# One fixed place for the split weights, and the next stage's first two blocks rounded and parted in four more tails

## What is computed

```
x = first_block(x, p, ...)
for i in range(4):
    h = modulate(rmsnorm(x, norm_g[i]), shift, scale)
    y = conv_branch(h) | rwkv_mixer(h) | attn_mixer(h)     # i = 0 and 3 | 1 | 2
    x = x + gate * y
return rmsnorm(x, final_g)
```

## Time and profile before

| | us |
|---|---|
| median of three runs | 3019.34 |
| lowest, highest | 3016.89, 3021.15 |
| the profiled execution: its own time | 3007.58 |
| its span, first to last instruction | 3005.8 |
| PE busy (28252 matmuls) | 2610.2 (87%) |
| PE weight loads | 2028.2 (67%) |
| DVE busy | 1748.8 (58%) |
| ACT busy | 1122.0 (37%) |
| POOL busy | 776.2 (26%) |
| mean granted clock of PE, share of full speed | 0.936 |

### The profile page before, as it was taken

How to read it: one execution, slowest core, us unless ns; L and a number is a source line. 1 busy time by engine, 2 the same in 40 slices (tenths; PEclk the granted TensorE clock), 3 DMA queues, 4 the chain that set the end, 5 groups by cost and what they waited for, 6 DMA issues and landing times. The chain is left out here.

```text
span 3005.8 us, 65971 instructions
## 1 busy us (share of the span) xinstructions
PE 2610.2 (87%) x28252; PEld 2028.2 (67%) x28252; DVE 1748.8 (58%) x2951; ACT 1122.0 (37%) x1751; POOL 776.2 (26%) x437
## 2 busy tenths in 40 slices
PE   7896879998599997788888888678999999898987
PEld 5774658776487686677677777567778755476755
DVE  4646978977822675454554554354771066535995
ACT  4531332223333422444444443332442344333323
POOL 2322210001122123644444452122332300032111
PEclk9998989989698898899999999889999999999998
DMA  4214424432234455111111100324332200033431
GB/s 149 77 43 133 161 71 118 111 93 91 97 107 151 157 188 182 40 36 45 51 40 46 51 25 14 122 91 147 133 126 64 84 1 1 1 119 92 136 94 56
DMA packets 83662, 266.34 MB, mean 89 GB/s; under 512 B 11824, under 2 KB 12848, under 8 KB 82992
## 3 DMA queue, kind: packets, MB, share of 16 engines
q1 hardware_dynamic: 74160, 236.97, 24.8%
q10 hardware_dynamic: 9216, 25.17, 2.1%
HBM read 203.04 MB, written 36.70 MB: 80 GB/s over the span
## 5 line engine op out<-in xcount | busy, mean ns | idle before, releaser
L358 PE MATMUL ps<-h_parts_conv,w_parts_conv 128*128 128x512 f32 x3936 | 766.5, 356 | 83.7 <-DVE h_parts_conv L344 47.6
L358 PEld LDWEIGHTS ps<-h_parts_conv,w_parts_conv 128*128 128x128 f32 x3936 | 643.2, 193 | 212.9 <-issue 54.7
L358 PE MATMUL ps<-scratch_scan 64*64 64x64 f32 (+1 forms) x15936 | 379.8, 239 | 82.9 <-issue 44.5
L358 PEld LDWEIGHTS ps<-scratch_scan 64*64 64x64 f32 x15936 | 342.9, 140 | 127.5 <-issue 83.6
L355 ACT ACTIVATE scratch_scan<-ps 128x384 f32<-128x384 f32 x560 | 241.0, 493 | 370.5 <-PE ps L358 228.4
L358 PE MATMUL ps<-h_parts_attn,w_parts_attn 128*128 128x512 f32 (+1 forms) x1536 | 330.5, 374 | 19.9 <-DVE h_parts_attn L352 12.3
L352 DVE SCALAR_TENSOR_TENSOR scratch_conv<-scratch_conv,vec 128x256 f32<-128x256 f32 (+1 forms) x672 | 335.2, 572 | 0.5
L358 PEld LDWEIGHTS ps<-h_parts_attn,w_parts_attn 128*128 128x128 f32 x1536 | 264.6, 191 | 78.6 <-issue 15.2
L432 POOL TENSOR_TENSOR w_parts_conv<-ring,w_parts_conv 128x1024 fp32r<-128x1024 f32 x50 | 131.4, 2629 | 592.2 <-ACT w_parts_conv L355 592.2
L358 PE MATMUL ps<-h_parts_block,w_parts_block 128*128 128x512 f32 x960 | 243.7, 414 | 38.5 <-POOL w_parts_block L432 27.7
L358 PEld LDWEIGHTS ps<-h_parts_block,w_parts_block 128*128 128x128 f32 x960 | 189.4, 200 | 92.4 <-issue 42.8
(11 more groups left out here) (206 smaller groups left out, 3586.0 us busy)
## 6 DMA issues: line engine op xcount, KB each, us to landing
ring<-in_weights SPq DMA_DIRECT2D x311, 512.0 KB, 3.7
rwkv_spill<-scratch_conv ACTq DMA_DIRECT2D x64, 384.0 KB, 2.3
stream<-rwkv_spill SPq DMA_DIRECT2D x64, 384.0 KB, 4.0
scratch_conv<-scratch_conv SPq DMA_DIRECT2D x128, 103.1 KB, 2.2
scratch_conv<-scratch_conv SPq DMA_DIRECT2D x128, 67.4 KB, 2.0
x_spill<-stream SPq DMA_DIRECT2D x2, 3072.0 KB, 9.7
y_spill<-scratch_scan SPq DMA_DIRECT2D x8, 384.0 KB, 4.0
scratch_rwkv_out<-y_spill SPq DMA_DIRECT2D x8, 384.0 KB, 6.5
```

What stands on the lines that cost most here:

```text
L358: return nc.tensor.matmul(o, l, r, start=start, stop=stop)
```

## The change

The split weights get a scope of their own, opened before everything else, so that they lie at one address. Only a stage with `split=False` (the scan) closes it; the stage after it opens it again. The softmax stage's scratch gets smaller by the size of the split weights (4096 elements per partition), since they now stay in place through it. With that, gate1, rwkvout, attn and attnout round (ACT) and part (POOL) the first two blocks of the next dense stage as well: their limits rise by two. The calls at the head of conv0, attn, attnout and conv1 stay in the code and find nothing left to do.

```diff
-        kept_scope, area_scope, parts_scope = (ctx.enter_context(ExitStack()) for _ in range(3))
+        w_scope, kept_scope, area_scope, parts_scope = (ctx.enter_context(ExitStack()) for _ in range(4))
...
             area_scope.close()
+            if not split:
+                w_scope.close()
+                PARTS.pop("W")
+            elif "W" not in PARTS:
+                weight_parts(name)
...
-            PARTS["W"] = ap(parts_scope.enter_context(nc.sbuf_tensor(f"w_parts_{name}", [P, 2, 2, DT * P], F32R)))
+        def weight_parts(name):
+            PARTS["W"] = ap(w_scope.enter_context(nc.sbuf_tensor(f"w_parts_{name}", [P, 2, 2, DT * P], F32R)))
...
+        weight_parts("one")
...
-                part_block(g, PSTART["gate1"] + DT)
+                part_block(g, PSTART["gate1"] + DT + 2)
...
-                    round_block(a, PSTART["gate1"] + min(m + 3, DT))
+                    round_block(a, PSTART["gate1"] + m + 3)
...
-        add_products("rwkvout", TT, lambda m, c: MODL[:, 1, 16 + m, c:c + 1], 0,
+        add_products("rwkvout", TT, lambda m, c: MODL[:, 1, 16 + m, c:c + 1], 2,
...
-        limit = PSTART["attnout"]
+        limit = PSTART["attnout"] + 2
...
-        area("parts", "softmax", SPLIT)
+        area("parts", "softmax", SPLIT - 4 * DT * P)
...
-                        round_block(a, min(PSTART["attnout"] + 2 * m + half + 3, PSTART["conv1"]))
+                        round_block(a, PSTART["attnout"] + 2 * m + half + 3)
...
-                part_block(g, PSTART["conv1"])
+                part_block(g, PSTART["conv1"] + 2)
```

## The result

The change made the kernel slower: 3028.24 us, median of 11 runs (3024.07 to 3038.84), against 3019.40 us of before (11 runs, 3016.89 to 3022.25); ratio 1.0026, 95% interval 1.0016 to 1.0037. The prediction said 3019.2 and a range up to 3025.5. The profiled execution after took 3033.27 us (span 3031.5).

The account below looks back on a forecast made before the run. PE, busy in 87% of the span, sets the pace in dense stages; the change moves its stops between stages. Tails 13.8 less heads 13.9 is -0.1 us, so 3019.2 on the runs' scale, range 3012.5 to 3025.5.

Parts of the forecast that it names:

- The fixed address and the smaller softmax scratch change no instruction: nothing: Whole kernel: the new place of the split weights and the smaller softmax scratch cost 0 us.
- The heads: Starts of conv0, attn, attnout, conv1: without two roundings and two partings each, 2.8, 3.0, 5.5, 2.6 saved, 13.9 us together.
- Conv1's head: Start of conv1: PE's third slice at 2744.0 in place of 2746.54, 2.6 us saved.
- the memset alone: Starts of conv0 and conv1: POOL's memset moves up against DVE's first low parts and costs nothing there.
- The tails: Ends of gate1, rwkvout, attn, attnout: added roundings and partings cost 3.7, 2.9, 3.9, 3.3, together 13.8 us.
- the 0.6 for the clock: End of rwkvout: PE's four sums take 2.93 in place of 2.32 us after a longer stop, 0.6 added.
- the clock's share: Start of softmax: PE's first 8 matmuls may run at half clock, 1.8 us more, of which 1.0 was taken.
- The tails are nearly free: Rival, all four tails: they cost 1.0, 1.0, 2.9 and 1.0 us, giving -8.0 and 3011.3; chance 0.13.
- The longer stops cost PE its clock: Rival, softmax's start, attnout's head, first dense blocks of conv0, attn, conv1: half clock, +6.3 us, 3025.6; chance 0.12.
- The blocks aren't there in time: Rival, end of gate1: a rounding waits for its load, one load late giving +3.7 us, 3023; chance 0.03.

Follow-up runs that it names:

- two gaps: Kernel after with 192 empty bytes behind the split weights and 64 ahead of attnout's split inputs, all stages aligned to 256: 3016.97 us, ratio 1.0008 to before.
- the gap of 64 in the kernel before: Kernel before with 64 empty bytes between split inputs and split weights, nothing else changed: ratio 1.0048 to before.
- the placement alone: Kernel after with all four added preparations undone, only the new fixed place of the split weights kept: 3023.86 us beside 3015.86 of before, ratio 1.0023.
- the aligned one: Kernel after without its four preparations, with 448 empty bytes behind the split weights and 576 ahead of attnout's split inputs: ratio 1.0007 to before.
- the second profile of before: Kernel before run once more unchanged for another profile: 3018.21 us.
- the two kernels after with a gap of 64 or 448: Kernel after with 64 or 448 empty bytes behind the split weights: ratios 1.0026 and 1.0009 to before.

## Why the prediction was wrong

**The step that failed** is the one sentence "The fixed address and the smaller softmax scratch change no instruction: nothing". It is true that they change no instruction, and it doesn't follow that they cost nothing. Timed alone they cost 0.23% [0.12, 0.35] of about 3016, some 7 us; with the distance mended 0.07% [-0.06, 0.19]. The same from the other side: the kernel after goes from 1.0026 to 1.0008 with two gaps, some 5 us of its 8.8. An upper estimate of the size comes from the rows: 44.51 less 44.10 over 192 is 2.1 ns for a matmul of 512. Blocks of 512 columns with a bad distance are 72 (in1, out1, gate1, conv1, convout1) and 32 in attn; 104 x 24 matmuls x 2.1 ns are 5.2 us. In attn's 16 wider blocks a pair of 512 and 256 takes some 1.5 ns longer (352.0 and 352.3 in the two kernels with the bad distance, 350.5 to 350.9 in before and the aligned ones, each the mean of a profile), 0.6 us. Together 5.8, if PE sets the pace all through; the 74 wider blocks of the other stages are left out, since their pace has two values of its own (below). For the gap of 64 in the kernel before, the same working (6.6 ns, attnout's 16 blocks too, 2.5 ns a pair in attn) gives 20, of which 14.5 were measured. PE does not set the pace everywhere: conv1's last dense product ends 164.45 us behind the stage's start in the placement alone and 164.30 in the aligned one, where its 576 matmuls at 2.1 ns would make 1.2 us.

**The heads** were right in sum. The timelines of the placement alone and of the kernel after, and those of the same two aligned, agree on it. Conv0's last dense product comes 2.9 us sooner behind the stage's start (2.8 said), in both pairs; attnout's comes 5.5 and 5.6 sooner (5.5 said), conv1's 1.9 and 2.0 (2.6 said), and attn's first product 3.1 (3.0 said). Together that is 13.5 in place of 13.9. Conv1's head was mis-sized by 0.7: POOL's building of the diagonals comes forward too (2766.31, behind the memset) and holds DVE's first low part for 1.38 us in place of 0.74. The prediction counted the memset alone and not what POOL does next. The stage times are a poorer measure: conv0 as a whole is 2.8 shorter in the aligned pair and 0.3 longer in the other, all of it behind its dense products, and of the 4.3 that conv1 to convout1 gained only 1.4 to 1.9 are in conv1; the rest lies in the two stages behind it, in which no instruction changed.

**The tails** came out at 13.8, as said, with errors that cancel; that is luck in part. Gate1 cost 3.5 to 3.7 by the stage times (3.7 said). Attnout cost 3.7 (3.3 said), by its timeline after against the aligned placement alone: from DVE's addition of the last product to PE's sums 4.93 and 2.20 us, and for the sums 2.07 and 1.13. Rwkvout cost 2.2 to 2.3 by the stage times (2.9 said), and the term that failed is the 0.6 for the clock: the sums took 2.93 after the longer stop, but without preparation, after the same stop of 3.23, they took 2.32 only in the first profile of before:

```profile
2011.50 2.93 PE L358 MATMUL ps<-scratch_rwkv_out,con 128*128 128x512 f32 x4 [3.23 <-DVE scratch_rwkv_out L344]
```

That is the second profile of before; the other kernels without this preparation have 2.27 to 2.93. At the start of softmax PE stood 3.92 us in place of 0.94, 3.0 more (2.9 said), and the clock's share was 1.2 us (1.0 said; 2.1 in the two kernels after with a gap of 64 or 448). The twentieth reduction of DVE in softmax starts 64.93 us behind PE's first product before and 66.09 after, and the distance between the two kernels is the same all the way from the fortieth matmul on:

```profile
2462.05 0.96 DVE L2827 TENSOR_REDUCE scratch_softmax<-ps 128x1 f32<-128x768 f32 x1 [5.05 <-PE ps L358]
```

```profile
2490.90 0.96 DVE L2836 TENSOR_REDUCE scratch_softmax<-ps 128x1 f32<-128x768 f32 x1 [5.05 <-PE ps L366]
```

Here the clock did fall: in the 4.2 us from 2424.8 on the granted clock was 0.72 and then 0.50, where before had 1.00. Attn with softmax should have grown by 0.9 in all (3.9 less 3.0); it grew by 7.2 in the pair that isn't aligned and by 0.4 in the aligned one. The softmax stage grew alike in both (2.4 and 2.3), so it is attn's own length that isn't settled: 4.8 longer in one pair, 1.9 shorter in the other.

**The rivals.** "The tails are nearly free" fell with the row of rwkvout. "The longer stops cost PE its clock" gave 3025.6, closer to the time than the forecast, but for the wrong reason, and that it came closer is luck: the granted clock over the whole span is 0.933 after and 0.933 in the second profile of before, and the aligned kernel, with the same stops, has no loss above 0.2%. "The blocks aren't there in time" fell too: loads land after 3.7 us as before, and no rounding in these tails waits for a load behind the last product.

**What the forecast could have seen.** The trace of before alone shows one distance class only, so no row of it priced the others. But the change moved W against H in every dense stage, PE is busy in 87% of the span and mostly with that pair, and the cost was set at nothing with no bound above. Even 0.5% left open on PE's 2610 us is 13 us, and the range would have held the time.

**What stays open.** How much of the 7 us each stage has: single profiles of the placement alone and of the aligned one differ by 1.6 us in their spans, less than the scan alone varies. Why the distance counts, and whether other pairs of operands have such classes; steps under 64 bytes weren't tried. In the stages with blocks of 768 columns there is a second thing: a pair of 512 and 256 takes 346.7 or 353.4 ns in the same stage of the same kernel (rwkvout in the two profiles of before). Other kernels of class 0 show either value there, and the two of class 64 both show 353.3. Whether class 64 costs a chance of the faster value, and what picks it, isn't shown.

## What to carry to other kernels

A move of a buffer is an edit of the hot loop: before calling a new layout free, write down the byte distance between the two operands that the busiest engine reads, before and after, modulo 256, and compare the time of one long unbroken run of it in both traces. An engine's preparation for the next stage belongs behind the last thing in the tail that it can hold up: the same rounding and parting that cost 2 to 4 us per tail showed no cost in rwkvout and attnout a few instructions later, under the sums and the root. And one profile of a kernel with a spread of 0.5% is a poor base for stage differences; a second one settled here what was chance.

## What the runs showed of the hardware

- TensorE's pace in a stream of 512-column matmuls depends on the distance of weights and moving data in a partition, modulo 256 bytes: 226.7, 229, 232.4 and 233.3 ns at 0, 64, 128 and 192, whichever of the two lies above (45.18 us for 192 in both orders), at full granted clock. It was 44.09 or 44.10 in all eight profiles of class 0. The Trainium skill (SBUF — State Buffer, "SBUF: two separate sides") says that on the engines' side only the port pair that DVE and GpSimd share causes contention, and that PE never waits on anyone. By that sentence alone the layout would cost PE nothing; the measured 0.9 to 2.9%, with nothing changed but the distance of PE's own two operands, say otherwise, and the measurement decides. What PE waits for there isn't shown.
- POOL's building of the diagonals (128 x 384) holds DVE as a parting does: in conv1 after, 1.38 us for a low part that takes 0.74 alone. In conv0 after, DVE's low part began 0.06 us ahead of POOL's second one (395.08 against 395.14); there DVE took its 0.74 and POOL 1.38 in place of 0.83.
- PE's four sums in rwkvout took 2.27 to 2.93 us after one and the same stop of 3.23, and 2.32 and 2.93 in two executions of the kernel before: the length of the stop alone doesn't tell how slow they are.
